# Column sums of the stick-breaking attention: operands rounded in two parts, and softplus at the end of the head's own step

## The chip, the cores and the metric

One core of one Trainium2 chip runs the whole program in one launch. The metric is the device time of an execution in microseconds, less is better. TensorE multiplies, ScalarE (ACT) evaluates functions, VectorE (DVE) does elementwise work, GpSimd (POOL) helps with small jobs, and SyncE (SP) issues the weight transfers.

## What is computed

Two blocks over 256 tokens of width 1024: an LRU layer, a sliding-window attention layer, a feed-forward layer, a mixer of MoBA and stick-breaking attention, a second feed-forward layer and a norm. The change lies in the stick-breaking attention of 8 heads:

```python
z = jnp.einsum('bhqd,bhsd->bhqs', qc, k).astype(jnp.float32) * scale
past = s_pos[None, :] < t[:, None]
log_fail = jnp.where(past, jax.nn.log_sigmoid(-z), 0.0)
later = lax.cumsum(log_fail, axis=3, reverse=True) - log_fail
w = jnp.where(past, jnp.exp(jax.nn.log_sigmoid(z) + later), 0.0)
return jnp.einsum('bhqs,bhsd->bhqd', w.astype(v.dtype), v)
```

With softplus(z) = max(z, 0) + log(1 + exp(-|z|)), the weight is exp(z - sum of softplus over the keys from s on).

## The kernel before

All weights stream through two staging buffers in halves of 128 x 1024 numbers. ScalarE rounds a half to the one-pass format fp32r (`w_hi`), VectorE makes the remainder (`w_lo`), and TensorE makes three products: hi x hi, hi x lo and lo x hi (L528: 24 instructions a half). The ring has 4 slots, so the half that is rounded after TensorE has finished half j is j + 4.

The stick-breaking heads are woven into the last sixteen halves of the mixer's input projection. A loop over steps r is written out on TensorE, ScalarE and VectorE alike. `STICK_FILL` says how many halves stand in each step (1, 2, 2, 1, 1, 2, 1, 1, 2, 1, 0, 2, 0); ScalarE and VectorE treat the halves of step r - 1 in step r. Keys lie on partitions. A head has 384 columns (`SC`): 256 queries against the first 128 keys, then the second 128 queries against the second 128 keys.

Step r on each engine, before:

- TensorE: in even steps the scores of heads r and r + 1 (L1004, L1007). Then the sums of head n = r - 2: a product of a lower triangle of ones with softplus (L1018, 384 columns) and of a square of ones with its last 128 columns (L1019), both plain fp32. They wait for softplus of head n (`sp_done`) and, since the bank is that of head n - 2, for that head's subtraction (`d_done`). In even steps from 6 on the values of heads r - 6 and r - 5. Then the step's halves.
- VectorE: the scores of head r with the mask into `stick_z(r)` (L2112); softplus of head r - 1 (L2119), which waits for ScalarE's logarithm; z less the sums of head r - 3 (L2124); then the halves' work (a projection's output, L1607, and the weight remainder, L1535), which waits for ScalarE's rounding.
- ScalarE: absolute value, exponential and logarithm of head r, the exponential of head r - 3, and the rounding of the halves (all recorded under L1055).

Each engine does its instructions in the order written; only semaphores tie them. GpSimd scales MoBA's probabilities (`normalise`, L493) ahead of this stretch. The constants lie in `con`, plain fp32, and `ones` is a square of ones.

Of the kernel before, what the change touches and what calls it, by code (L numbers as in the profile page):

```python
# [7 lines left out]
F32 = mybir.dt.float32  # L8
# [3 lines left out]
ALU = mybir.AluOpType  # L12
# [3 lines left out]
P = 128  # L16
T = 256
TB = T // P
D = 1024
KD = D // P  # L20
# [8 lines left out]
NH = 8  # L29
# [6 lines left out]
SC = T + P  # L36
# [40 lines left out]
IDENT, TRI, DIST, CMASK, SBMASK, FREQ = 0, 128, 256, 512, 768, 1152  # L77
# [20 lines left out]
def fill(counts, first, r):  # L98

    return range(first + sum(counts[:r]), first + sum(counts[:r + 1]))  # L100
# [57 lines left out]
def build(nc, I, out):  # L158
    ctx = ExitStack()
    with ctx:  # L160
        def sb(name, shape, dt=F32):
            return ctx.enter_context(nc.sbuf_tensor(name, shape, dt))

        def sem(name):
            return ctx.enter_context(nc.semaphore(name))
# [7 lines left out]
        acts = sb("acts", [P, 30, 2, T], F32R)  # L173
# [8 lines left out]
        con = sb("con", [P, N_CONST])  # L182
        ones = sb("ones", [P, P])
# [23 lines left out]
        bank = [two[b // 2][:, b % 2, :] for b in range(8)]  # L207

        def tiles(t, n=1):

            return arena[:, t:t + n, :].rearrange("p t n -> p (t n)")
# [23 lines left out]
        xn_ready, xh_ready, xl_ready = sem("xn_ready"), sem("xh_ready"), sem("xl_ready")  # L235
# [23 lines left out]
        rope_turn, rope_out = sem("rope_turn"), sem("rope_out")  # L259
        z_done, z_sb, sb_abs, sb_exp, sb_ln, sp_done, c_done, d_done, w_exp = (  # L260
            sem(n) for n in ("z_done", "z_sb", "sb_abs", "sb_exp", "sb_ln", "sp_done", "c_done", "d_done", "w_exp"))
        ym_hi, ym_lo, g_sig = sem("ym_hi"), sem("ym_lo"), sem("g_sig")
        br_done, mg_a, mg_b, mg_f, mg_hi, mg_lo = (
            sem(n) for n in ("br_done", "mg_a", "mg_b", "mg_f", "mg_hi", "mg_lo"))
# [25 lines left out]
        def score_parts(n, sinks):  # L290

            s = score_buf(n)
            return [s[:, 0:P + sinks], s[:, P + 1:SC + 1 + sinks]]
# [10 lines left out]
        def stick_z(n):  # L304

            return flat[:, 48 * T + (n % 6) * SC:48 * T + (n % 6 + 1) * SC]

        def stick_sp(n):

            return flat[:, 24 * T + (n % 2) * SC:24 * T + (n % 2 + 1) * SC]  # L310

        def stick_ln(n):

            return flat[:, 27 * T + (n % 3) * SC:27 * T + (n % 3 + 1) * SC]
# [118 lines left out]
        def _(pool):  # L433
# [55 lines left out]
            def normalise(n):  # L489

                pool.wait_ge(den_inv, n + 1)
                for q, s in enumerate(score_parts(n, 0)):
                    pool.tensor_scalar(s, s, rden[:, 2 * n + q:2 * n + q + 1], 1.0, ALU.mult, ALU.mult).then_inc(p_norm, 1)  # L493
# [22 lines left out]
                .then_inc(fin_gain_in, 16)  # L516
            for h in range(NH):
                normalise(NQ + h)


        @block.tensor
        def _(pe):
# [318 lines left out]
            def values_of_two(n, o, v, w):  # L841

                c = (n // 2 % 2) * T
                for i in range(2):
                    pe.matmul(bank[o][i * HD:(i + 1) * HD, c:c + T], v[i][0], w[i][:, 0:T], start=True, stop=False,  # L845
                              skip_group_check=True)
                for i in range(2):
                    pe.matmul(bank[o][i * HD:(i + 1) * HD, c + P:c + T], v[i][1], w[i][:, T:SC], start=False, stop=True,
                              skip_group_check=True).then_inc(o_done, 1)
# [12 lines left out]
            for r in range(NQ + LAG + 2):  # L862
# [4 lines left out]
                if r >= LAG + 2 and (r - LAG) % 2:  # L867
                    n = r - LAG - 3
# [91 lines left out]
            for j in range(12):  # L960
# [5 lines left out]
                if j in MIX_TURN:  # L966
                    n = MIX_TURN[j]
# [11 lines left out]
            for r in range(NH + LAG + 2):  # L979
                n = NQ + r  # L980
# [4 lines left out]
                if r >= LAG + 2 and (r - LAG) % 2:  # L985
                    h = r - LAG - 3
# [10 lines left out]
            for r in range(NH + 5):  # L997
                if r < NH and r % 2 == 0:
                    if r >= 2:
                        pe.wait_ge(z_sb, r)  # L1000
                    q, k = tiles(8 + r // 2), tiles(12 + r // 2)
                    for i in range(2):
                        s = slice(i * HD, (i + 1) * HD)
                        pe.matmul(bank[i][:, 0:T], k[s, 0:P], q[s, 0:T], start=True, stop=True)  # L1004
                    for i in range(2):
                        s = slice(i * HD, (i + 1) * HD)
                        pe.matmul(bank[i][:, T:SC], k[s, P:T], q[s, P:T], start=True, stop=True).then_inc(z_done, 1)  # L1007
                if r == 2:
                    pe.wait_ge(t_out, NQ + NH)
                if r == 5:  # L1010
                    pe.wait_ge(m_val, 4)
                if 2 <= r < NH + 2:
                    n = r - 2
                    pe.wait_ge(sp_done, n + 1)
                    if n >= 2:
                        pe.wait_ge(d_done, n - 1)
                    sums, sp_n = bank[2 + n % 2], stick_sp(n)
                    pe.matmul(sums[:, 0:SC], con[:, TRI:TRI + P], sp_n, start=True, stop=False, skip_group_check=True)  # L1018
                    pe.matmul(sums[:, P:T], ones[:, :], sp_n[:, T:SC], start=False, stop=True, skip_group_check=True)\  # L1019
                        .then_inc(c_done, 1)  # L1020
                if r >= 5 and r % 2 == 0:
                    h = r - 6
                    pe.wait_ge(w_exp, h + 2)
                    if h % 4 == 0:
                        pe.wait_ge(ym_lo, h // 4 + 1)
                    values_of_two(h, 6 + h // 4,
                                  [[v[:, tb * 512 + i * HD:tb * 512 + (i + 1) * HD] for tb in range(TB)] for i in (h, h + 1)],
                                  [stick_z(h), stick_z(h + 1)])
                for j in fill(STICK_FILL, 24, r):
                    mix_half(j)  # L1030
# [496 lines left out]
        def _(dve):  # L1527
            def lo(n, i=0, step=0):

                if n >= half_of(C_END):  # L1530
                    return
                src, landed, count = source(n)
                w = src.shape[-1]
                dve.wait_ge(hi_done, n + 1 + i * step)
                dve.tensor_tensor(w_lo[:, n % RING, 0:w], src, w_hi[:, n % RING, 0:w].bitcast(F32), ALU.subtract)\  # L1535
                    .then_inc(w_done, 1)
# [20 lines left out]
            def root_inv(n):  # L1557
                dve.wait_ge(std_ready, n + 1)
                dve.reciprocal(n_rstd[:, :], n_std[:, :]).then_inc(rstd_ready, 1)
# [35 lines left out]
            def roots_out(n, b=3):  # L1595

                dve.wait_ge(rb_ready, n)
                dve.tensor_copy(spread[:, :], bank[b][:, 0:T]).then_inc(rb_sb, 1)
                dve.wait_ge(rb_sb, n)
# [97 lines left out]
            for n in range(half_of(C_G)):  # L1697
                if n - 1 in x_end:
                    xb_lo(x_end[n - 1])
                if n in x_end:  # L1700
                    c = x_end[n]
                    dve.wait_ge(conv_b, 2 * c + 2)
                    for tap in range(1, CONV):
                        for m in range(2):
                            t = 2 * c + m
# [363 lines left out]
            def mix_slot(j):  # L2069

                c = j // 2
                if j == 3:
                    root_inv(3)
                if j == 4:
                    dve.wait_ge(rstd_ready, 4)
                    mix_out(0)
                    rope(0)
                    mix_out(1)
                if j == 5:
                    rope(1)  # L2080
                    roots_out(3)
                if j == 8:
                    mix_out(2)
                    rope(2)
                    mix_out(3)
                if j == 9:
                    rope(3)
                if j % 2 and c >= 6 and c not in (10, 11):
                    mix_out(c)
                lo(H_M + 4 + j)  # L2090
# [16 lines left out]
            for r in range(NH + 5):  # L2107
                if r < NH:
                    dve.wait_ge(z_done, r + 1)
                    if r >= 6:  # L2110
                        dve.wait_ge(o_done, NQ + NH + r - 5)
                    dve.tensor_tensor(stick_z(r), bank[r % 2][:, 0:SC], con[:, SBMASK:SBMASK + SC], ALU.add)\  # L2112
                        .then_inc(z_sb, 1)
                if 1 <= r <= NH:
                    n = r - 1
                    dve.wait_ge(sb_ln, n + 1)
                    if n >= 2:
                        dve.wait_ge(c_done, n - 1)
                    dve.scalar_tensor_tensor(stick_sp(n), stick_z(n), 0.0, stick_ln(n), ALU.max, ALU.add)\  # L2119
                        .then_inc(sp_done, 1)  # L2120
                if 3 <= r < NH + 3:
                    n = r - 3
                    dve.wait_ge(c_done, n + 1)
                    dve.tensor_tensor(stick_z(n), stick_z(n), bank[2 + n % 2][:, 0:SC], ALU.subtract).then_inc(d_done, 1)  # L2124
                if r >= 1:
                    for j in fill(STICK_FILL, 24, r - 1):
                        mix_slot(j)
                if r == 9:
                    branch_lo(2)
            for j in fill(STICK_FILL, 24, NH + 4):  # L2130
# [110 lines left out]
```

## Time and profile before

| | us |
|---|---|
| median of 3 runs | 810.54 (810.51 to 810.54) |
| the profiled execution | 810.75 |
| its span | 809.0 |
| TensorE busy | 796.4 |
| VectorE busy | 572.6 |
| ScalarE busy | 487.2 |
| GpSimd busy | 89.4 |

The span is that of the profiled execution; 1.75 us of its time lie around it. Busy times of matmuls overlap, since matmuls are pipelined: the time from one start to the next tells what one costs. A wait is idle time of an engine just before an instruction, put down to what released it. A plain fp32 matmul shows as two instructions, one on fp32r as one. Start times are microseconds from the start of the span.

### The profile page before, as it was taken

How to read it: one execution, taken by the hardware profiler on the slowest of the kernel's cores; microseconds unless marked ns; L12 is line 12 of the kernel's file. 1: busy time of each engine (PE TensorE's matmuls, PEld its weight loads, DVE VectorE, ACT ScalarE, POOL GpSimd, SP SyncE). 2: the span in 40 equal slices, each digit the busy share in tenths (PEclk: the TensorE clock that was granted, in tenths of full speed). 3: DMA queues.
4: the chain of work that ended last, by engine and by line, in shares of the span. 5: the costliest groups of instructions: out<-in, count | busy, mean ns of one | idle time of the engine just before them, and what ended most of it. 6: DMA issues, size and time to landing. Idle time of an engine off the chain costs nothing.

```text
span 809.0 us, 15016 instructions
## 1 busy us (share of the span) xinstructions
PE 796.4 (98%) x5557; PEld 728.5 (90%) x5557; DVE 572.6 (71%) x860; ACT 487.2 (60%) x763; POOL 89.4 (11%) x152
## 2 busy tenths in 40 slices
PE   8999999999999999999999999999999999999997
PEld 8999999988898888889998899988999888888885
DVE  5987897976687977786449655556587787877443
ACT  6779956886566655554346456655747565555343
POOL 9405100057400000000000012000000000000000
PEclk9999999999999999999999999999999999999999
DMA  8624565643355766665565545344546576665651
GB/s 266 203 93 127 166 204 183 184 139 97 105 183 156 209 185 204 184 184 196 186 181 174 171 132 163 106 146 155 163 152 181 166 227 186 181 191 181 198 181 53
DMA packets 101045, 136.31 MB, mean 169 GB/s; under 512 B 5064, under 2 KB 86400, under 8 KB 100992
## 3 DMA queue, kind: packets, MB, share of 16 engines
q1 hardware_dynamic: 99232, 133.23, 54.0%
q0 software_dynamic: 1600, 2.28, 1.0%
q8 instruction: 36, 0.59, 0.3%
q14 instruction: 17, 0.14, 0.1%
q10 hardware_dynamic: 160, 0.07, 0.0%
HBM read 134.51 MB, written 1.05 MB: 168 GB/s over the span
## 4 chain that ended last, share of the span: by engine, by line
PE 90%; DVE 5%; ACT 3%; issue 1%; DMA 0%; ACTq 0%; DVEq 0%
PE bank L528 40%; PE bank L597 17%; PE bank L594 10%; PE bank L536 8%; PE bank L641 7%; PE bank L592 2%; DVE w_lo L1535 2%; ACT w_hi L1055 1%; PE bank L825 1%; PE bank L845 1%; ACT arena L1055 1%; PE bank L838 1%; ACT acts L1055 1%; PE bank L1018 1%; DVE arena L1870 1%
## 5 line engine op out<-in xcount | busy, mean ns | idle before, releaser
L1535 DVE TENSOR_TENSOR w_lo<-stage,w_hi 128x1024 fp32r<-128x1024 f32 x249 | 303.2, 1224 | 156.6 <-ACT w_hi L1055 155.9
L528 PE MATMUL bank<-acts,w_hi 128*128 128x256 f32 (+1 forms) x1936 | 353.6, 285 | 2.1 <-DVE arena L1710 0.6
L1055 ACT ACTIVATE w_hi<-stage 128x1024 fp32r<-128x1024 f32 (+1 forms) x251 | 261.5, 1049 | 96.0 <-PE bank L528 48.5
L528 PEld LDWEIGHTS bank<-acts,w_hi 128*128 128x128 f32 x1936 | 301.2, 192 | 7.2 <-issue 4.3
L528 PE MATMUL bank<-acts,w_lo 128*128 128x256 f32 (+1 forms) x968 | 273.7, 283 | 0.0
L597 PE MATMUL bank<-acts,w_hi 128*128 128x512 f32 x616 | 217.6, 396 | 0.0
L594 PE MATMUL bank<-acts,w_lo 128*128 128x256 f32 x704 | 189.7, 280 | 0.0
L528 PEld LDWEIGHTS bank<-acts,w_lo 128*128 128x128 f32 x968 | 185.5, 192 | 0.0
L597 PEld LDWEIGHTS bank<-acts,w_hi 128*128 128x128 f32 x616 | 115.7, 188 | 25.5
L594 PEld LDWEIGHTS bank<-acts,w_lo 128*128 128x128 f32 x704 | 132.7, 188 | 3.6
L1055 ACT ACTIVATE arena<-bank 128x512 f32<-128x512 f32 (+1 forms) x79 | 44.1, 558 | 69.2 <-PE bank L597 46.4
L536 PE MATMUL bank<-w_hi,acts 128*128 128x256 f32 (+1 forms) x320 | 71.6, 319 | 0.4 <-DVE w_lo L1535 0.4
L1055 ACT ACTIVATE arena<-arena 128x512 f32<-128x512 f32 (+3 forms) x64 | 38.5, 605 | 46.9 <-DVE arena L1982 19.2
L493 POOL TENSOR_SCALAR arena<-arena,rden 128x128 f32<-128x128 f32 (+1 forms) x48 | 29.0, 616 | 293.4 <-DVE rden L1880 293.1
L1055 ACT ACTIVATE acts<-arena 128x512 fp32r<-128x512 f32 (+3 forms) x41 | 26.3, 642 | 57.5 <-DVE arena L2003 32.2
L536 PEld LDWEIGHTS bank<-w_hi,acts 128*128 128x128 f32 x320 | 52.3, 191 | 4.1 <-DVE w_lo L1535 0.5
L641 PE MATMUL bank<-w_hi,acts 128*128 128x512 f32 x176 | 54.5, 390 | 0.0
L536 PE MATMUL bank<-w_lo,acts 128*128 128x256 f32 (+1 forms) x160 | 50.4, 315 | 0.0
L1974 DVE TENSOR_TENSOR arena<-arena,bank 128x512 f32<-128x512 f32 x44 | 30.2, 686 | 23.2 <-ACT arena L1055 23.2
L641 PEld LDWEIGHTS bank<-w_hi,acts 128*128 128x128 f32 x176 | 33.0, 188 | 6.8
L1055 ACT ACTIVATE arena<-arena,ntop 128x129 f32<-128x129 f32 (+3 forms) x48 | 21.4, 448 | 21.3 <-DVE ntop L1873 21.2
L641 PE MATMUL bank<-w_lo,acts 128*128 128x512 f32 x88 | 34.2, 389 | 0.0
(188 smaller groups left out, 686.3 us busy)
## 6 DMA issues: line engine op xcount, KB each, us to landing
stage<-ffn_w_gate SPq DMA_DIRECT2D x44, 512.0 KB, 4.4
stage<-ffn_w_up SPq DMA_DIRECT2D x44, 512.0 KB, 4.5
stage<-ffn_w_down SPq DMA_DIRECT2D x44, 512.0 KB, 3.6
stage<-w_in SPq DMA_DIRECT2D x40, 512.0 KB, 3.6
stage<-a_w_in SPq DMA_DIRECT2D x24, 512.0 KB, 4.6
stage<-b_w_in SPq DMA_DIRECT2D x16, 512.0 KB, 3.8
stage<-a_w_out SPq DMA_DIRECT2D x12, 512.0 KB, 3.6
stage<-b_w_out SPq DMA_DIRECT2D x8, 512.0 KB, 3.5
```

The costliest lines, as they stand in the source:

```text
L493: pool.tensor_scalar(s, s, rden[:, 2 * n + q:2 * n + q + 1], 1.0, ALU.mult, ALU.mult).then_inc(p_norm, 1)
L528: mm = pe.matmul(dst, w[:, slot, c:c + P], a[:, k, :] if isinstance(k, int) else a[:, bass.ds(k, 1), :], start=start and n == 0, stop=stop ...
L536: mm = pe.matmul(dst, a[:, k, tb * P:(tb + 1) * P], w[:, slot, c:c + n], start=start and i == 0, stop=stop and i == 2, skip_group_check=True)
L592: pe.matmul(two[p][:, m, :], w_hi[:, half % RING, c:c + P], wide(acts[:, k, :, :]), start=True, stop=False, skip_group_check=True)
L594: mm = pe.matmul(two[p][:, m, 0:T], w_lo[:, half % RING, c:c + P], a_hi[:, k, :], start=False, stop=False, skip_group_check=True)
L597: mm = pe.matmul(two[p][:, m, :], w_hi[:, half % RING, c:c + P], wide(acts[:, k, :, :]), start=False, stop=k == KD - 1, skip_group_check=True)
L641: mm = pe.matmul(token_bank(tb, h)[:, :], a[:, k, t], w[:, slot, c], start=False, stop=w is w_hi and a is a_hi, skip_group_check=True)
L825: mm = pe.matmul(bank[i][:, c:c + w], q[r, t * T + c:t * T + c + P], k[r, 0:keys], start=True, stop=True)
L838: mm = pe.transpose(bank[2 + n % 2][:, c * P:(c + 1) * P], p[:, at:at + P], ident)
L1055: return nc.scalar.activation(out_, in_, func, **kw)
L1535: dve.tensor_tensor(w_lo[:, n % RING, 0:w], src, w_hi[:, n % RING, 0:w].bitcast(F32), ALU.subtract)\
L1974: dve.tensor_tensor(y, y, two[ffn_two(n, j, u)][:, :, 0:T], ALU.add).then_inc(ff_add, 1)
```

## The change

1. `stick_two(n)` gives two fp32r buffers of 384 columns in `acts` for each of two heads in turn. VectorE writes softplus rounded into the first (a copy) and the remainder into the second (a subtraction).
2. Softplus, copy and subtraction of head r stand at the end of VectorE's step r, behind the halves' work. Softplus of head r - 1 no longer stands behind the masking in step r.
3. TensorE makes the sums of a head from four fp32r matmuls: triangle and square by the rounded part (after `sp_hi`), then by the remainder (after `sp_lo`).
4. GpSimd makes fp32r copies of the triangle and of the ones once, behind the scaling of MoBA's first head.

```diff
+        def stick_two(n):
+
+            two_parts = acts[:, 16 + 2 * (n % 2):18 + 2 * (n % 2), :, :].rearrange("p k s t -> p (k s t)")
+            return two_parts[:, 0:SC], two_parts[:, SC:2 * SC]
+
+        tri, all_ones = acts[:, 24, 0, 0:P], acts[:, 24, 0, P:T]
...
             for h in range(NH):
                 normalise(NQ + h)
+                if h == 0:
+                    pool.wait_ge(xl_ready, KD * 5)
+                    pool.tensor_copy(tri, con[:, TRI:TRI + P]).then_inc(tri_in, 1)
+                    pool.tensor_copy(all_ones, ones[:, :]).then_inc(tri_in, 1)
...
                 if 2 <= r < NH + 2:
                     n = r - 2
-                    pe.wait_ge(sp_done, n + 1)
+                    if n == 0:
+                        pe.wait_ge(tri_in, 2)
+                    pe.wait_ge(sp_hi, n + 1)
                     if n >= 2:
                         pe.wait_ge(d_done, n - 1)
-                    sums, sp_n = bank[2 + n % 2], stick_sp(n)
-                    pe.matmul(sums[:, 0:SC], con[:, TRI:TRI + P], sp_n, start=True, stop=False, skip_group_check=True)
-                    pe.matmul(sums[:, P:T], ones[:, :], sp_n[:, T:SC], start=False, stop=True, skip_group_check=True)\
+                    sums, (sp_h, sp_l) = bank[2 + n % 2], stick_two(n)
+                    pe.matmul(sums[:, 0:SC], tri, sp_h, start=True, stop=False, skip_group_check=True)
+                    pe.matmul(sums[:, P:T], all_ones, sp_h[:, T:SC], start=False, stop=False, skip_group_check=True)
+                    pe.wait_ge(sp_lo, n + 1)
+                    pe.matmul(sums[:, 0:SC], tri, sp_l, start=False, stop=False, skip_group_check=True)
+                    pe.matmul(sums[:, P:T], all_ones, sp_l[:, T:SC], start=False, stop=True, skip_group_check=True)\
                         .then_inc(c_done, 1)
...
-                if 1 <= r <= NH:
-                    n = r - 1
-                    dve.wait_ge(sb_ln, n + 1)
-                    if n >= 2:
-                        dve.wait_ge(c_done, n - 1)
-                    dve.scalar_tensor_tensor(stick_sp(n), stick_z(n), 0.0, stick_ln(n), ALU.max, ALU.add)\
-                        .then_inc(sp_done, 1)
                 if 3 <= r < NH + 3:
                     n = r - 3
                     dve.wait_ge(c_done, n + 1)
...
                 if r >= 1:
                     for j in fill(STICK_FILL, 24, r - 1):
                         mix_slot(j)
+                if r < NH:
+                    n = r
+                    dve.wait_ge(sb_ln, n + 1)
+                    if n >= 2:
+                        dve.wait_ge(c_done, n - 1)
+                    sp_h, sp_l = stick_two(n)
+                    dve.scalar_tensor_tensor(stick_sp(n), stick_z(n), 0.0, stick_ln(n), ALU.max, ALU.add)\
+                        .then_inc(sp_done, 1)
+                    dve.wait_ge(sp_done, n + 1)
+                    dve.tensor_copy(sp_h, stick_sp(n)).then_inc(sp_hi, 1)
+                    dve.wait_ge(sp_hi, n + 1)
+                    dve.tensor_tensor(sp_l, stick_sp(n), sp_h.bitcast(F32), ALU.subtract).then_inc(sp_lo, 1)
```

VectorE in steps 3 and 4 before (a row is an instruction, `x2` two of them; L2112 masking, L2119 softplus, L2124 the subtraction of the sums, L1607 a projection's output, L1535 a weight remainder):

```order
495 L2112 TENSOR_TENSOR arena<-bank,con 128x384
496 L2119 SCALAR_TENSOR_TENSOR arena<-arena 128x384
497 L2124 TENSOR_TENSOR arena<-arena,bank 128x384
498 L1607 TENSOR_TENSOR arena<-bank,spread 128x512
499 L1535 TENSOR_TENSOR w_lo<-stage,w_hi 128x1024 x2
500 L2112 TENSOR_TENSOR arena<-bank,con 128x384
501 L2119 SCALAR_TENSOR_TENSOR arena<-arena 128x384
502 L2124 TENSOR_TENSOR arena<-arena,bank 128x384
```

The same place after (L2129 masking, L2134 subtraction of the sums, L1624 output, L1552 weight remainder, L2144 softplus, L2147 the rounding copy, L2149 its remainder):

```order
503 L2129 TENSOR_TENSOR arena<-bank,con 128x384
504 L2134 TENSOR_TENSOR arena<-arena,bank 128x384
505 L1624 TENSOR_TENSOR arena<-bank,spread 128x512
506 L1552 TENSOR_TENSOR w_lo<-stage,w_hi 128x1024 x2
507 L2144 SCALAR_TENSOR_TENSOR arena<-arena 128x384
508 L2147 CAST acts<-arena 128x384
509 L2149 TENSOR_TENSOR acts<-arena,acts 128x384
510 L2129 TENSOR_TENSOR arena<-bank,con 128x384
511 L2134 TENSOR_TENSOR arena<-arena,bank 128x384
```

Softplus went from between masking and subtraction to behind the weight remainders, with two instructions more behind it and the next masking after them.

TensorE in step 4 before, scores of heads 4 and 5 and the sums of head 2:

```order
2092 L1004 MATMUL bank<-arena 128x256 x2
2093 L1007 MATMUL bank<-arena 128x128 x2
2094 L1018 MATMUL bank<-arena,con 128x384
2095 L1019 MATMUL bank<-arena,ones 128x128
2096 L528 MATMUL bank<-acts,w_hi 128x256 x2
```

The same place after (L1016 and L1019 the scores, L1032 to L1036 the sums, L540 the projection):

```order
2096 L1016 MATMUL bank<-arena 128x256 x2
2097 L1019 MATMUL bank<-arena 128x128 x2
2098 L1032 MATMUL bank<-acts 128x384
2099 L1033 MATMUL bank<-acts 128x128
2100 L1035 MATMUL bank<-acts 128x384
2101 L1036 MATMUL bank<-acts 128x128
2102 L540 MATMUL bank<-acts,w_hi 128x256 x2
```

Two matmuls of a head's sums became four, at the same place between the scores and the step's halves.

## Rows read from the trace of the kernel before

**Rows 1.** The page: busy time of TensorE, and the chain that ended last, by engine

```profile
PE 796.4 (98%) x5557; PEld 728.5 (90%) x5557; DVE 572.6 (71%) x860; ACT 487.2 (60%) x763; POOL 89.4 (11%) x152
...
PE 90%; DVE 5%; ACT 3%; issue 1%; DMA 0%; ACTq 0%; DVEq 0%
```

**Rows 2.** Waits of TensorE from 505 to 580 us: who, for whom, total, times, longest

```profile
PEld bank L1018 <- DVE arena L2119: 1.1, 1, 1.1
PE bank L1018 <- DVE arena L2124: 0.9, 1, 0.9
```

**Rows 3.** Timeline of VectorE, 508 to 575 us: start, duration, engine, line, operation

```profile
513.15 0.56 DVE L2119 SCALAR_TENSOR_TENSOR arena<-arena 128x384 f32<-128x384 f32 x1 [1.42 <-ACT arena L1055]
...
519.07 0.56 DVE L2112 TENSOR_TENSOR arena<-bank,con 128x384 f32<-128x384 f32 x1 [2.12 <-PE bank L1007]
...
524.65 0.55 DVE L2112 TENSOR_TENSOR arena<-bank,con 128x384 f32<-128x384 f32 x1
...
530.64 0.55 DVE L2112 TENSOR_TENSOR arena<-bank,con 128x384 f32<-128x384 f32 x1
...
534.35 1.23 DVE L1535 TENSOR_TENSOR w_lo<-stage,w_hi 128x1024 fp32r<-128x1024 f32 x1 [1.63 <-ACT w_hi L1055]
535.49 0.55 DVE L2112 TENSOR_TENSOR arena<-bank,con 128x384 f32<-128x384 f32 x1
...
543.79 0.56 DVE L2112 TENSOR_TENSOR arena<-bank,con 128x384 f32<-128x384 f32 x1 [3.36 <-PE bank L848]
...
549.78 0.55 DVE L2112 TENSOR_TENSOR arena<-bank,con 128x384 f32<-128x384 f32 x1
550.25 0.55 DVE L2119 SCALAR_TENSOR_TENSOR arena<-arena 128x384 f32<-128x384 f32 x1
550.72 0.55 DVE L2124 TENSOR_TENSOR arena<-arena,bank 128x384 f32<-128x384 f32 x1
```

**Rows 4.** Timeline of ScalarE, same stretch

```profile
513.03 1.07 ACT L1055 ACTIVATE arena<-arena 128x384 f32<-128x384 f32 x2
...
514.65 1.04 ACT L1055 ACTIVATE w_hi<-stage 128x1024 fp32r<-128x1024 f32 x1
```

**Rows 5.** The chain that ended last, 500 to 585 us: start, duration, piece

```profile
526.71 2.86 PE bank L528 x24
...
534.36 0.65 PE bank L1018 x2
535.00 0.22 PE bank L1019 x2
...
541.82 0.84 PE bank L1018 x2
...
551.41 0.88 PE bank L1018 x2
```

**Rows 6.** The same view, 700 to 809 us

```profile
743.70 59.87 PE bank L641 x264
```

**Rows 7.** VectorE: one-source scalings (groups), and a dependent pair (timeline)

```profile
L1624 DVE TENSOR_SCALAR arena<-arena,n_rstd 128x256 f32<-128x256 f32 x5 | 1.8, 396 | 0.0
...
L2208 DVE TENSOR_SCALAR arena<-arena,n_rstd 128x512 f32<-128x512 f32 x2 | 1.0, 488 | 0.1
...
591.62 0.42 DVE L2154 TENSOR_TENSOR arena<-arena,bank 128x256 f32<-128x256 f32 x1 [1.22 <-PE bank L528]
592.15 0.42 DVE L2161 TENSOR_TENSOR arena<-arena 128x256 f32<-128x256 f32 x1
```

**Rows 8.** The program's end: TensorE's last matmul (timeline), the granted clock (windows)

```profile
803.16 0.39 PE L641 MATMUL bank<-w_hi,acts 128*128 128x512 f32 x1
...
core 0: us, PE busy (x) PEld busy (x) DVE busy (x) ACT busy (x) POOL busy (x), PEclk, DMA share, GB/s
...
805.00:806.00 1.00, 0.00 (x0) 0.00 (x0) 0.56 (x3) 0.72 (x1) 0.00 (x0) 0.77 0.79 293
806.00:807.00 1.00, 0.00 (x0) 0.00 (x0) 0.00 (x0) 0.00 (x0) 0.00 (x0) 0.50 0.30 113
```

**Rows 9.** Timeline of TensorE at the program's start

```profile
1.01 3.78 PE L703 MATMUL bank<-ones 128*128 128x128 f32 x16 [1.01 <-POOL half_pi L436]
```

**Rows 10.** Timeline of GpSimd, 455 to 510 us, the second scaling

```profile
476.19 0.83 POOL L493 TENSOR_SCALAR arena<-arena,rden 128x128 f32<-128x128 f32 x2 [3.15 <-DVE rden L1880]
```

More of the change, by code:

```diff
@@ L261, in build @@
             sem(n) for n in ("z_done", "z_sb", "sb_abs", "sb_exp", "sb_ln", "sp_done", "c_done", "d_done", "w_exp"))
+        sp_hi, sp_lo, tri_in = sem("sp_hi"), sem("sp_lo"), sem("tri_in")
         ym_hi, ym_lo, g_sig = sem("ym_hi"), sem("ym_lo"), sem("g_sig")
```

## Prediction

> **What bounds the kernel now.** Read the page first: TensorE is busy for 98% of the span and carries 90% of the chain that ended last [rows 1]. So an edit counts by what it does to TensorE: the work it takes off, and the waits it makes. Next, the waits of TensorE in the stick-breaking stretch (505 to 580 us): all that is there is one wait of 0.9 us at the sums of one head, noted under matmul and weight load, its end being head 4's subtraction (L2124) on VectorE [rows 2]. Third, VectorE's timeline there: VectorE and ScalarE go through the steps in lockstep. From one masking (L2112) to the next it takes 4.85 us in a step with one weight half (530.64 to 535.49) and 5.99 us with two (524.65 to 530.64) [rows 3]. In between VectorE idles 1.6 us for ScalarE, which does three functions of the head and the rounding of a half first. TensorE's own work of a step is about as long: a half is 2.87 us [rows 5].
>
> **TensorE's part.** A head's sums are two fp32 matmuls now, each two instructions: 0.65 + 0.22 = 0.87 us in a stream, 0.84 + 0.22 right behind the score matmuls [rows 5]. After, there are four one-instruction matmuls of rounded operands. Their rate is that of the main products: 2.86 / 24 = 0.119 us for 256 columns [rows 5], 59.87 / 264 = 0.227 us for 512 [rows 6]; half way, 0.173 us for 384. No row shows 128 columns of this kind. Extending the line gives 0.065; L1019's instructions take 0.22 / 2 = 0.11; four passes, as fp32 takes, would be 0.22. I take 0.11, the row with the same weights to load. A head costs 2 x (0.173 + 0.11) = 0.57 us, 0.30 us less (bounds 0.39 less and 0.08 less). If nothing else moved: 8 x 0.30 = 2.4 us off.
>
> **VectorE's part.** Each head gets a rounding copy and a subtraction, and softplus (the old L2119) moves from the next step's head, where it lay in the 1.6 us wait for ScalarE, to the end of its own step, where nothing covers it: the next masking stands behind it in VectorE's queue. The subtraction has two sources and 384 columns, as L2112 and L2119: 0.55 us, 0.47 to the next start (549.78 and its neighbours) [rows 3]. The copy has one source. The nearest rows are scalings of 256 columns, 0.396 us, and of 512, 0.488 us [rows 7]; midway is 0.44, and both also read a column of scalars, which the copy does not. I take 0.40, with 0.35 and 0.55 (a two-source operation of that width) as bounds. The three depend on each other; a dependent operation starts 0.11 us after its forerunner ends (591.62 + 0.42, then 592.15) [rows 7]. The tail of a step is T = (0.55 + 0.11) + (0.40 + 0.11) + 0.47 = 1.64 us.
>
> The Trainium skill (VectorE: DVE Perf Modes, its perf-mode tier table) says that an fp32 tensor_copy in SBUF runs at two elements a cycle. By that the copy would be about 0.36 us (an estimate), T 1.60, and the result 0.3 us lower. No row here shows a plain copy within SBUF.
>
> **Following the queue.** The first step has no weight half, so VectorE stands until ScalarE has head 0's logarithm at 513.15 [rows 3], as it does now, but with head 1's masking behind it.
> - Head 1 is masked at 513.15 + T = 514.79.
> - To head 2: masking 0.58, ScalarE's three functions and a half 513.03 to 515.69 = 2.66 [rows 4], 0.03, the remainder of a weight half 1.14 (534.35 to 535.49) [rows 3], T: 520.84, against 519.07.
> - To heads 3, 4, 5, 6 and 7: the present distances 5.58, 5.99, 4.85, 4.85 and 5.99 [rows 3], each plus T, since softplus did not lengthen a step before and the tail now does: 528.06, 535.69, 542.18, 548.67, 556.30. The distance now from head 5 to head 6 is longer, but that is a wait for TensorE's head 0 and 1 outputs, which come before 547.
> - Head 4's subtraction from the sums ends 1.02 later.
>
> That is 545.84 + 7T = 557.32 us, where it is 551.27 now (550.72 + 0.55) [rows 3]: **6.05 us later**. TensorE's sums of head 6 wait for exactly this, since they take the bank of head 4. On the way head 3's sums wait for head 1's subtraction, which ends at 535.69 + 1.02 = 536.71; TensorE would be there at 534.36 - 3 x 0.30 = 533.5 [rows 5], so it stands for 3.4 us, some 1.0 us more at head 5, and 4.0 us at head 6. The five savings before that vanish in these waits; only those of heads 6 and 7 stay, 0.60 us. Behind head 6 no wait on VectorE is left (head 7 needs head 5's subtraction at about 563, TensorE comes at 565), and everything later hangs on TensorE: 6.05 - 0.60 = **+5.45 us**.
>
> GpSimd's two casts stand behind the first head's scaling, where it now idles 3.15 us [rows 10]; each is about 0.4 us, like its 128-column scalings: nothing. The earlier release of softplus is worth nothing either: no TensorE wait ends on it. No transfer moves past another; the stage loads follow the weight remainders, still ahead of TensorE.
>
> **The clock.** At the end of the program TensorE's last matmul runs to 803.55 (803.16 + 0.39); the granted clock of 805 to 806 is 0.77 and then 0.50, the 1.2 GHz level [rows 8], so it fell some 2.0 us after TensorE went quiet. No wait of TensorE in the middle of the program is over 1 us now; the new ones are 3.4 and 4.0. So I expect a fall in them. One at head 3 is paid out of the later waits. One at head 6 is not: TensorE is then alone on the path. Its price: at the start sixteen fp32 instructions of 128 columns take 3.78 us, 0.236 each [rows 9], against 0.11 [rows 5], and the pace is full only after some 6 us. Between 0 and half of that, 3 us, I take 1.5. The Trainium skill (TensorE: Matmul & The Clock Gate, the table "Why this matters for your kernels") also warns of idle gaps between bursts of matmuls; it and the rows of the end agree.
>
> **Sum.** The profiled execution took 810.75 us, span 809.0; the median of the runs is 810.54. 810.75 + 5.45 + 1.5 = 817.7, and 817.5 against the median.
>
> **Rivals.**
> - The loop as above, but the clock holds or falls where it costs nothing: 816.0. For it: the clock stays at 1.00 through every short gap now. Against it: the end of the trace. 0.25.
> - The loop is longer: copy at 0.55 us (7 x 0.15 = 1.0 more) or a slow stretch of up to 3 us: 819 to 821. 0.12. The matmuls of 128 columns at 0.22 us belong here: 2 x 2 x 0.11 = 0.4 more.
> - The tail costs less than it adds up to: dependent starts cost 0.03 us instead of 0.11, as from ScalarE to VectorE, and ScalarE catches part of the later masking up: 811 to 814. 0.08.
> - Faster, 808.1: the steps have room for the tail, and TensorE's 2.4 us come through. The place is head 4's subtraction, the point 545.84 + 7T = 551.27 + 0.60, so T = 0.86 us. Softplus and the subtraction alone are 0.94, without copy or dependence. TensorE waits at that point already. 0.03.
> - The change doesn't do what it says: rounded operands run in four passes like fp32. Then a head costs 1.74 us, 0.87 more, of which heads 6 and 7 count, 2.3 more than in the sum: 819 to 820. Against it: 0.119 us for 256 columns. 0.04.
>
> The forecast, 817.5, has 0.48, its own range 816.5 to 819. The range 814.5 to 820.5 leaves out the cheap-tail and faster cases and the far end of the long ones. A measurement of this kernel tells about 0.2% (1.6 us) from no change: faster by more 0.03, within it 0.04, slower 0.93.
>
> **What would show it.** In the profile after: the masking's starts 6.5 us (one half) and 7.6 us (two) apart in place of 4.85 and 5.99; copy 0.40 and subtraction 0.55 us; head 4's subtraction ending about 6 us later; waits of TensorE at the first sums matmul of heads 3 and 6, 3 to 4 us each, released by VectorE's subtraction from the sums; sums of a head in 0.57 us; a granted clock below 1.00 in the slices at 535 to 565 us. It is wrong if these waits are absent (VectorE had room), if T is under 1 us, or if the clock stays 1.00, which is the first rival.

## The result

| | before | after |
|---|---|---|
| median | 810.54 us (6 runs) | 816.33 us (6 runs, 815.12 to 817.51) |
| ratio after / before | | 1.007, 95% interval 1.006 to 1.008 |
| profiled execution, span | 810.75, 809.0 us | 815.13, 813.3 us |

The kernel became 0.7% slower. TensorE's busy time rose by 0.5 us, although its added matmuls are cheaper than those removed, and the granted clock left full speed in the middle of the program. Of all the runs behind this document one, of the kernel "The old place" below, took 960.15 us at a mean granted clock of 0.753; it is left out of every median and ratio. From the page of after, the busy time and the clock in the 40 slices (the row of before has nines from end to end):

```profile
PE 796.9 (98%) x5557; PEld 730.8 (90%) x5557; DVE 579.3 (71%) x876; ACT 487.3 (60%) x763; POOL 90.2 (11%) x154
...
PEclk9999999999999999999999999989999999999999
```

VectorE's timeline in the stick-breaking stretch, after: the tail of the first step, then the masking of each head (L2129) in turn and head 4's subtraction (L2134), which answer to [rows 3]:

```profile
512.99 0.56 DVE L2144 SCALAR_TENSOR_TENSOR arena<-arena 128x384 f32<-128x384 f32 x1 [1.89 <-ACT arena L1072]
513.58 0.36 DVE L2147 CAST acts<-arena 128x384 fp32r<-128x384 f32 x1
513.97 0.56 DVE L2149 TENSOR_TENSOR acts<-arena,acts 128x384 fp32r<-128x384 f32 x1
514.45 0.55 DVE L2129 TENSOR_TENSOR arena<-bank,con 128x384 f32<-128x384 f32 x1
...
520.34 0.55 DVE L2129 TENSOR_TENSOR arena<-bank,con 128x384 f32<-128x384 f32 x1
...
527.37 0.55 DVE L2129 TENSOR_TENSOR arena<-bank,con 128x384 f32<-128x384 f32 x1
...
534.81 0.55 DVE L2129 TENSOR_TENSOR arena<-bank,con 128x384 f32<-128x384 f32 x1
...
541.11 0.55 DVE L2129 TENSOR_TENSOR arena<-bank,con 128x384 f32<-128x384 f32 x1
...
547.83 0.56 DVE L2129 TENSOR_TENSOR arena<-bank,con 128x384 f32<-128x384 f32 x1 [0.33 <-PE bank L860]
...
555.28 0.55 DVE L2129 TENSOR_TENSOR arena<-bank,con 128x384 f32<-128x384 f32 x1
555.75 0.54 DVE L2134 TENSOR_TENSOR arena<-arena,bank 128x384 f32<-128x384 f32 x1
```

The maskings of heads 2 to 5 are 7.03, 7.44 and 6.30 us apart, where they were 5.58, 5.99 and 4.85. Each step grew by 1.45 us: 0.59 for softplus, 0.39 for the copy, 0.47 for the subtraction up to the next start. Head 4's subtraction ends at 556.29 (555.75 + 0.54), 5.02 us later than before. The stretch itself began 0.17 us earlier (the first masking, not among these lines, starts at 510.55; before it was 510.72), so 5.19 us were lost up to there.

TensorE's waits on that subtraction's line (500 to 600 us: who, for whom, total, times, longest), in answer to [rows 2], and pieces of the chain, in answer to [rows 5]:

```profile
PE bank L1032 <- DVE arena L2134: 4.9, 2, 2.7
```

```profile
535.97 0.66 PE bank L1032
...
556.44 0.41 PE bank L1032
...
563.95 0.18 PE bank L1032
564.12 0.06 PE bank L1033
564.18 0.23 PE bank L1035
564.41 0.06 PE bank L1036
```

Two waits, 2.7 us at head 3 and 2.2 at head 6. A head's sums at full speed are 0.18 + 0.06 + 0.23 + 0.06 = 0.53 us (from 563.95). At head 3 the first matmul behind the wait is 0.66 us long, at head 6 0.41: at head 3 the array was slow. The windows (stretch; busy time and instructions of TensorE, its weight loads, VectorE, ScalarE, GpSimd; then the granted clock) show where:

```profile
530.00:534.00 4.00, 3.31 (x28) 3.10 (x26) 2.89 (x4) 1.99 (x3) 0.00 (x0) 1.00 0.16 32
534.00:538.00 4.00, 2.03 (x8) 2.06 (x9) 2.39 (x5) 2.54 (x5) 0.00 (x0) 0.69 0.77 245
538.00:542.00 4.00, 4.00 (x21) 4.00 (x20) 3.42 (x6) 0.79 (x2) 0.00 (x0) 0.50 0.20 54
542.00:546.00 4.00, 4.00 (x35) 3.82 (x33) 1.30 (x3) 2.72 (x5) 0.00 (x0) 0.96 0.22 77
552.00:556.00 4.00, 2.23 (x19) 2.03 (x17) 3.93 (x7) 0.60 (x2) 0.00 (x0) 1.00 0.46 144
556.00:560.00 4.00, 3.56 (x29) 3.15 (x30) 1.91 (x3) 2.89 (x5) 0.00 (x0) 1.00 0.33 120
```

TensorE stood idle from about 533.3 to 536, and the clock is 0.50 from 538 to 542, the 1.2 GHz level, with 21 matmuls in 4 us instead of some 35. In this execution the wait at head 6 (552 to 556) passed without a fall.

### The profile page after: what moved, and what is told of

Its sections match the earlier page's. It is cut to its first block, busy times and chain, and to the rows that moved or that the text cites. A ratio compares the mean times of both kernels' runs of the same rounds, so it can differ in the third digit from the quotient of the medians.

```text
span 813.3 us, 15034 instructions
## 1 busy us (share of the span) xinstructions
PE 796.9 (98%) x5557; PEld 730.8 (90%) x5557; DVE 579.3 (71%) x876; ACT 487.3 (60%) x763; POOL 90.2 (11%) x154
## 4 chain that ended last, share of the span: by engine, by line
PE 89%; DVE 6%; ACT 3%; issue 1%; DMA 0%; ACTq 0%; DVEq 0%
PE bank L540 39%; PE bank L609 17%; PE bank L606 10%; PE bank L548 8%; PE bank L653 7%; PE bank L604 2%; DVE w_lo L1552 2%; ACT w_hi L1072 1%; ACT arena L1072 1%; PE bank L837 1%; PE bank L857 1%; PE bank L850 1%; ACT acts L1072 1%; DVE arena L1887 1%; DMA rows_n<-a_norm_g 0%
## 5 line engine op out<-in xcount | busy, mean ns | idle before, releaser
L1552 DVE TENSOR_TENSOR w_lo<-stage,w_hi 128x1024 fp32r<-128x1024 f32 x249 | 302.9, 1223 | 158.6 <-ACT w_hi L1072 157.8
L540 PE MATMUL bank<-acts,w_hi 128*128 128x256 f32 (+1 forms) x1936 | 355.7, 286 | 2.0 <-DVE arena L1727 0.6
L540 PEld LDWEIGHTS bank<-acts,w_hi 128*128 128x128 f32 x1936 | 303.2, 193 | 7.1 <-issue 4.3
L540 PE MATMUL bank<-acts,w_lo 128*128 128x256 f32 (+1 forms) x968 | 274.8, 284 | 0.0
L540 PEld LDWEIGHTS bank<-acts,w_lo 128*128 128x128 f32 x968 | 186.6, 193 | 0.0
```

The costliest lines, as they stand in the source:

```text
L540: mm = pe.matmul(dst, w[:, slot, c:c + P], a[:, k, :] if isinstance(k, int) else a[:, bass.ds(k, 1), :], start=start and n == 0, stop=stop ...
```

## The experiments

Each kernel was timed beside the kernel before on the same chip; the ratios are to that. The three instructions at the end of VectorE's step (softplus, copy, remainder) are called the tail. Theory 1: what is lost is the tail, behind which the next masking queues, seven times up to head 4's subtraction, plus a fall of the clock in the waits that this makes. A run's mean clock is the granted clock over its whole span; a fall in mid-program lowers it, and so does a fall at the very end, so that the kernel before shows 0.998 to 1.000.

**Moving only.** Plain fp32 sums as before, softplus alone at the end of its own step.

```diff
-                if 1 <= r <= NH:
-                    n = r - 1
-                    dve.wait_ge(sb_ln, n + 1)
...
                     for j in fill(STICK_FILL, 24, r - 1):
                         mix_slot(j)
+                if r < NH:
+                    n = r
+                    dve.wait_ge(sb_ln, n + 1)
...
```

> The kernel before with its plain fp32 sums, softplus alone moved to the end of the head's own step. Theory 1: T is 0.47 us, head 4's subtraction could end at 545.84 + 7 x 0.47 = 549.1, earlier than 551.27, so the loop stays bound by TensorE as before: 810.5 us, within 0.5. Rival (the move by itself is what costs, by the wait for ScalarE in the first step): 812 to 814 us.

Measured: 810.64 us, ratio 1.0001 (0.9992 to 1.0009). The move by itself costs nothing; TensorE's only wait on VectorE in the stretch is still one of 0.9 us.

**The old place.** All of the rounding, at softplus's old place:

```diff
+                if 1 <= r <= NH:
+                    n = r - 1
+                    dve.wait_ge(sb_ln, n + 1)
...
+                    dve.tensor_tensor(sp_l, stick_sp(n), sp_h.bitcast(F32), ALU.subtract).then_inc(sp_lo, 1)
                 if 3 <= r < NH + 3:
                     n = r - 3
                     dve.wait_ge(c_done, n + 1)
...
-                if r < NH:
-                    n = r
-                    dve.wait_ge(sb_ln, n + 1)
...
```

> The rounded parts and the four one-pass matmuls as in the changed kernel, but softplus, copy and subtraction stand where softplus stood before, right behind the next head's masking, in VectorE's wait for ScalarE. Theory 1 (what costs is that the next masking queues behind the tail, once per step, 7T up to head 6): the maskings go back to 4.85 and 5.99 us apart, and the time is 810.5 - 0.7 = 809.8 us, with up to 1.7 more if the wait left at head 6 (2.5 us) lets the clock fall. Rival (the extra VectorE work costs wherever it stands): 815 us or more.

Measured: 811.59 us, ratio 1.0011 (1.0002 to 1.002); nine of twelve runs lie from 811.47 to 811.66, one at 810.02 and one at 812.80. So 4.7 of the 5.8 us are a matter of place. The maskings did not quite go back to the old distances. VectorE's timeline of step 4 of this kernel (L2129 masking, L2137 softplus, L2140 copy, L2142 its remainder, L2146 subtraction of the sums), and two windows behind head 6's wait:

```profile
530.82 0.55 DVE L2129 TENSOR_TENSOR arena<-bank,con 128x384 f32<-128x384 f32 x1
531.29 0.55 DVE L2137 SCALAR_TENSOR_TENSOR arena<-arena 128x384 f32<-128x384 f32 x1
531.87 0.36 DVE L2140 CAST acts<-arena 128x384 fp32r<-128x384 f32 x1
532.27 0.56 DVE L2142 TENSOR_TENSOR acts<-arena,acts 128x384 fp32r<-128x384 f32 x1
532.75 0.55 DVE L2146 TENSOR_TENSOR arena<-arena,bank 128x384 f32<-128x384 f32 x1
...
535.98 0.55 DVE L2129 TENSOR_TENSOR arena<-bank,con 128x384 f32<-128x384 f32 x1
```

```profile
552.00:554.00 2.00, 2.00 (x14) 1.43 (x13) 1.23 (x2) 0.74 (x1) 0.00 (x0) 0.63 0.23 88
554.00:556.00 2.00, 2.00 (x11) 2.00 (x11) 1.85 (x4) 0.05 (x1) 0.00 (x0) 0.52 0.36 72
```

The maskings are 5.16 us apart (530.82 to 535.98), not 4.85. The subtraction of the sums now comes behind the tail, ScalarE's exponential waits for it (0.18 us in this step), and its rounding of the half stands behind that: the cover is not wide enough by 0.3 us. This does not reach the end: head 6's masking waits for TensorE's values of heads 0 and 1 here (1.26 us) as before (3.36), and head 4's subtraction ends at 551.23, where it was 551.27. What brings the time above the kernel before is the clock: behind the wait of 2.5 us at head 6 it is 0.63 and 0.52. The run at 810.02 has a mean clock of 0.999, the nine one of 0.996 or 0.997, that at 812.80 one of 0.995. By that one run, this kernel without a fall is 0.6 us faster than the kernel before (810.63 on that chip); with it, it is 1.0 us slower.

**One place further on.** The tail behind the subtraction of the sums, ahead of the halves:

```diff
                     dve.tensor_tensor(stick_z(n), stick_z(n), bank[2 + n % 2][:, 0:SC], ALU.subtract).then_inc(d_done, 1)
+                if 1 <= r <= NH:
+                    n = r - 1
+                    dve.wait_ge(sb_ln, n + 1)
...
+                    dve.tensor_tensor(sp_l, stick_sp(n), sp_h.bitcast(F32), ALU.subtract).then_inc(sp_lo, 1)
                 if r >= 1:
                     for j in fill(STICK_FILL, 24, r - 1):
                         mix_slot(j)
```

> As e1, but softplus, copy and subtraction stand one place further on: behind the masking and the subtraction of the sums, ahead of the step's halves. Theory 1: neither the masking nor the subtraction of the sums waits for the tail, TensorE's saving comes through in part: 808.7 us, a wait of 1.7 us left at head 6, maskings 4.85 and 5.99 us apart. Rival: the tail takes time from the weight remainders behind it and TensorE waits for a half: 811 us or more.

Measured: 810.61 us, ratio 0.9994 (0.9985 to 1.0003), in two groups: three of eleven runs from 809.08 to 809.11 at a mean clock of 0.999, eight from 810.55 to 810.67 at 0.997. Two maskings one half apart, then the only wait of TensorE left on VectorE (L2144 is the rounding copy here), and two windows behind it:

```profile
530.48 0.55 DVE L2129 TENSOR_TENSOR arena<-bank,con 128x384 f32<-128x384 f32 x1
...
535.34 0.55 DVE L2129 TENSOR_TENSOR arena<-bank,con 128x384 f32<-128x384 f32 x1
```

```profile
PE bank L1032 <- DVE acts L2144: 1.5, 1, 1.5
```

```profile
550.00:552.00 2.00, 1.87 (x10) 1.15 (x12) 1.34 (x3) 1.78 (x3) 0.00 (x0) 0.75 0.74 276
552.00:554.00 2.00, 2.00 (x13) 1.67 (x10) 1.98 (x3) 0.46 (x2) 0.00 (x0) 0.50 0.03 12
```

The maskings are back at the distance of before (4.86 us, where it was 4.85), so the same 1.46 us cost nothing in this place. Even this short wait let the clock fall in the profiled execution, and a fall costs 1.5 us here (810.61 against 809.1). That was not expected: the forecast was 808.7 us, and the shortest pause I had a row for was 2.0 us.

**The clock.** 24 matmuls of 256 columns whose output nobody reads, right before the wait at the sums of head 3, of head 6, or of both (the diff shows both):

```diff
+                    if n in (3, 6):
+                        for _ in range(24):
+                            pe.matmul(bank[7][:, 0:T], tri, acts[:, 0, 0, :], start=True, stop=True, skip_group_check=True)
                     pe.wait_ge(sp_hi, n + 1)
```

> The changed kernel with 24 matmuls of 256 columns more, whose output nobody reads, right before the sums of head 3 and of head 6, so that TensorE works through 2.9 us of each long wait. Theory 1 (the spread of the changed kernel, 815.1 to 817.5, is the clock's fall in one of the two waits): clock 1.00 through the stretch, every run at 815.0 within 0.2. Rival (the spread has another cause, and the clock costs nothing): the same spread of over 2 us, or 2 x 2.9 us more.

> The changed kernel with the 24 unread matmuls only ahead of head 6's sums. Theory 1 (a fall of the clock in head 3's wait is paid out of the later waits, one in head 6's is not): every run at 814.8 to 815.2 us, with or without a fall at head 3. Rival (the fall at head 3 also counts): a spread up to 817.

> The changed kernel with the 24 unread matmuls only ahead of head 3's sums. Theory 1: head 6's wait of 3.8 us is left open, the clock falls there in most runs: 814.8 us where it does not, 816 to 817.5 where it does. Rival: steady at 815.

| unread matmuls before | median | lowest to highest, 5 runs |
|---|---|---|
| heads 3 and 6 | 814.82 us | 814.79 to 814.87 |
| head 6 only | 814.70 us | 814.63 to 814.76 |
| head 3 only | 816.49 us | 816.19 to 817.74 |
| none (the changed kernel, 6 runs) | 816.33 us | 815.12 to 817.51 |

Matmuls without use ahead of head 6's sums, with or without those at head 3, make the kernel faster by 1.5 to 1.6 us, and its five runs then lie within 0.13 us. The windows with head 6's wait filled:

```profile
534.00:538.00 4.00, 1.98 (x16) 2.01 (x17) 2.44 (x5) 2.49 (x5) 0.00 (x0) 1.00 0.78 251
...
552.00:556.00 4.00, 3.21 (x27) 3.01 (x26) 3.93 (x8) 0.60 (x2) 0.00 (x0) 1.00 0.51 174
556.00:560.00 4.00, 3.91 (x32) 3.49 (x33) 1.91 (x3) 2.54 (x5) 0.00 (x0) 1.00 0.23 90
```

and with only head 3's filled, ahead of them the waits of TensorE on VectorE in that kernel (L1035 is the first sums matmul, 3 lines further down):

```profile
PE bank L1035 <- DVE arena L2137: 4.4, 2, 3.8
```

```profile
534.00:538.00 4.00, 4.00 (x35) 4.00 (x34) 2.45 (x5) 2.45 (x5) 0.00 (x0) 1.00 0.79 251
...
552.00:556.00 4.00, 0.34 (x3) 0.14 (x2) 3.93 (x8) 0.60 (x2) 0.00 (x0) 0.99 0.57 175
556.00:560.00 4.00, 3.89 (x17) 2.98 (x18) 1.91 (x3) 2.56 (x5) 0.00 (x0) 0.50 0.24 89
560.00:564.00 4.00, 4.00 (x26) 4.00 (x25) 2.39 (x5) 1.47 (x2) 0.00 (x0) 0.66 0.46 131
```

Head 6's open wait is 3.8 us there, and the clock is 0.50 from 556 to 560. Filled, it stays 1.00. So a fall at head 6 costs 1.5 to 3.0 us where it comes (816.19 and 817.74, against 814.70). The runs of that kernel fit in the mean clock too: 0.997 from 816.19 to 816.49, 0.995 at 817.72 and 817.74.

With head 6's filled and head 3's open no run is over 814.76. In the profiled execution of that kernel the clock held at head 3 (534 to 538), and four of its five runs have a mean clock of 0.999, so the case of a fall at head 3 with head 6's wait filled was hardly tested. What such a fall costs is told by the changed kernel itself: its profiled execution has one and is among its lowest, 0.4 us above 814.70. Its head 6 masking then waited 0.33 us for TensorE's values of heads 0 and 1 (547.83 above).

The spread of the changed kernel is then a matter of where the clock falls. All its six runs have the same mean clock, 0.995, yet go from 815.12 to 817.51, 0.4 to 2.8 us above 814.70; the median is 1.6 above. That fits a fall at head 3 in the lowest and at head 6 in the others. But the one execution of it that was profiled fell at head 3; for the others the place is inferred, not seen.

**The length of the tail.** Once without the remainder (no subtraction, and its two matmuls left out, so a part of the computation is missing; the diff shows VectorE's part), once with the copy made twice:

```diff
-                    dve.wait_ge(sp_hi, n + 1)
-                    dve.tensor_tensor(sp_l, stick_sp(n), sp_h.bitcast(F32), ALU.subtract).then_inc(sp_lo, 1)
```

```diff
                     dve.wait_ge(sp_done, n + 1)
+                    dve.tensor_copy(sp_l, stick_sp(n))
                     dve.tensor_copy(sp_h, stick_sp(n)).then_inc(sp_hi, 1)
```

> The changed kernel without the remainder of softplus: no subtraction, and the two matmuls of it left out, so that a part of the computation is missing. The tail is 0.59 + 0.28 = 0.87 us. Theory 1 (time goes as 7 tails up to head 6): 7 x (1.46 - 0.87) = 4.1 us less than the changed kernel without a fall of the clock, 815.1 - 4.1 = 811.0, up to 2 more where the clock falls in head 6's wait. Rival (the loss is mostly one shift in the first step, where VectorE stands for the logarithm): 814 us.

> The changed kernel with the rounding copy made twice (the first into the remainder's buffer, overwritten afterwards). The tail grows by a copy's start distance of 0.28 us. Theory 1: 7 x 0.28 = 2.0 us more: 817.1 us at the least and up to 819.5 with the clock's fall. Rival: 0.3 us more or nothing, VectorE having 29% idle time.

Measured: 811.55 us without the remainder (ratio to before 1.0013, 1.0004 to 1.0022) and 818.41 with the second copy (1.0098, 1.0084 to 1.0111; lowest run 816.62). First and last masking of each, from VectorE's timeline:

```profile
510.67 0.55 DVE L2126 TENSOR_TENSOR arena<-bank,con 128x384 f32<-128x384 f32 x1
...
550.84 0.55 DVE L2126 TENSOR_TENSOR arena<-bank,con 128x384 f32<-128x384 f32 x1
```

```profile
510.84 0.55 DVE L2129 TENSOR_TENSOR arena<-bank,con 128x384 f32<-128x384 f32 x1
...
557.04 0.55 DVE L2129 TENSOR_TENSOR arena<-bank,con 128x384 f32<-128x384 f32 x1
```

From head 0's masking to head 7's it is 40.17 us without the remainder, 44.73 in the changed kernel, 46.20 with the second copy. The tails are 0.60 us shorter and 0.27 longer; seven of them are 4.2 less and 1.9 more. Found are 4.56 less and 1.47 more; what differs is 0.36 and 0.42. Neither kernel waits at head 6's masking, while in the changed kernel that wait put it off by 0.42 us (541.11 to 547.83 is 6.72, not 6.30). Without it the loop goes as seven tails, both ways, within 0.1 us.

The times bear it out. From the 814.70 without a fall, 1.9 more is 816.6, and the lowest run is 816.62; the expectation's "at the least 817.1" had started from 815.12, which holds a fall at head 3. The other way, 4.2 for the tails and 2 x 0.29 for the matmuls left out at heads 6 and 7 give 809.9; measured is 811.55, at mean clocks of 0.995 to 0.998 in all eleven runs, so one fall of 1.6 us would close the sum. The profiled execution (812.98) shows such a fall at head 6.

**A kernel that gains.** The tail as in the last place, and one half of the projection moved from step 8 to step 7, so that real work stands where the wait was; and the same half moved in the kernel before:

```diff
-STICK_FILL = [1, 2, 2, 1, 1, 2, 1, 1, 2, 1, 0, 2, 0]
+STICK_FILL = [1, 2, 2, 1, 1, 2, 1, 2, 1, 1, 0, 2, 0]
```

> As e4, and one half of the projection stands in step 7 instead of step 8, so that TensorE has 2.87 us of real work ahead of head 6's sums. Theory 1 (e4's 809.1 and 810.6 us are one wait of 1.6 us at head 6 and the clock's fall in it): the wait goes, no fall, 809.1 - 1.6 - up to 0.6 = 806.5 to 807.5 us in every run. Rival (the half moves the wait to another place, or VectorE's step 8 with its two halves becomes the bound): 808.5 us or more.

> The kernel before with only the same half moved from step 8 to step 7. Theory 1: its one wait of 0.9 us goes, 809.5 us; the gain of e7 over this one, some 3 us, is then TensorE's saving on the sums (8 x 0.34 = 2.7 us). Rival: most of e7's gain comes from the moved half alone: 807 to 808 us.

Measured: 807.04 us with the rounded sums, ratio 0.9961 (0.9948 to 0.9975), four of five runs from 807.00 to 807.06, one at 808.68 with a mean clock of 0.999, as high as that of the others (0.998 to 0.999), so not by the clock; 809.40 us for the kernel before with the half moved, ratio 0.9985 (0.9976 to 0.9994). The chain of the former has no wait at head 6 (551.43); the two halves ahead of it and the sums:

```profile
545.63 5.80 PE bank L540 x48
551.43 0.18 PE bank L1032
551.61 0.06 PE bank L1033
551.67 0.23 PE bank L1035
551.89 0.06 PE bank L1036
```

The half alone brings 1.2 us: its wait of 0.9 us, and the first sums matmul behind it, which takes 0.65 us in the stream instead of 0.88. The rounded sums bring a further 2.4 us, of the 8 x 0.34 = 2.7 that they save on TensorE (some 3 were expected). This version beats both kernels.

## Why the prediction was right, point by point

The time forecast was 817.5 us in a range of 814.5 to 820.5; it is 816.33. The direction and the mechanism held: VectorE's queue, with the next masking behind the tail, not TensorE's matmuls, sets the end of the stretch.

- **TensorE's part.** Forecast 0.57 us for a head's sums, measured 0.53. A 128-column matmul takes 0.06, the extension of the line, not the 0.11 I took; but the 384 columns behind it take 0.23 instead of 0.18. The pair is 0.29, where I had 0.28. The saving is 0.34 us a head instead of 0.30. The prediction speaks of five savings that vanish before head 6; there are six, heads 0 to 5. The sum has only those of heads 6 and 7 and is not touched by that.
- **The tail.** T was mis-sized: 1.64 us forecast, 1.46 measured. Two terms were off. A dependent instruction on VectorE starts 0.03 us after the end of its forerunner (512.99 + 0.56, then 513.58), not 0.11; the row I had taken reads `bank`, TensorE's output memory, and whether that makes the difference was not tested. And the copy is 0.36 us, not 0.40. The Trainium skill (VectorE: DVE Perf Modes, its perf-mode tier table) was right on that one: an fp32 copy within SBUF at two elements a cycle gives some 0.36 us (an estimate), and the trace agrees with 0.36.
- **Following the queue.** With T = 1.46 the formula 545.84 + 7T gives 556.06; less the earlier start of 0.17 and with the 0.42 by which the wait at head 6's masking put it off it is 556.31, measured 556.29. That wait I had ruled out, since I let a slow clock at head 3 be paid out of TensorE's waits alone. In this execution it also delayed the values of heads 0 and 1. The two experiments on the length of the tail bear the seven out.
- **What is left at the end.** The sum had +5.45 us without the clock. The profiled execution is 4.38 us above that of before (815.13 - 810.75), the filled kernel 4.2 above the median (814.70 - 810.54).
- **The clock.** Forecast a fall at head 6 for 1.5 us; the filled kernels show 1.6 in the median, and 0.4 to 3.0 in single runs. The 1.5 was the middle between nothing and 3 us, so that it came out so well is in part luck: single runs lie near both ends. In the profiled execution the fall is at head 3 and not at head 6. Luck also lies in the 2.0 us after which the clock fell at the end of the kernel before: at the end of the changed kernel TensorE's last matmul ends before 808 us, and the clock is still 1.00 up to 812. The prediction lets the Trainium skill (TensorE: Matmul & The Clock Gate, "Why this matters for your kernels") and the rows of the end agree; they do in kind, but its warning is for longer gaps than the 1.5 us that were enough here, and the measurement decides. The waits were forecast as 3.4 us at head 3, 1.0 at head 5 and 4.0 at head 6. They are 2.7 at head 3, shorter by four tails of 0.18 less each; where head 3's is filled, 0.6 at head 5 and 3.8 at head 6; and in the changed kernel's profiled execution none at head 5 and 2.2 at head 6, since TensorE came later by its slow stretch.
- **Rivals.** That the clock holds was the first, at 816.0. It gave the right time to 0.3 us for the wrong reason: without a fall the kernel is at 814.7. The sum was 1.2 us too high in the loop and right on the clock. Of the rival with a cheap tail (811 to 814) one half came true, the dependent starts at 0.03 us; it is worth 7 x 0.16 = 1.1 us. The other half did not: ScalarE caught nothing up, each step grew by the whole tail. The loop was not longer than forecast either, though in single runs a fall cost 3 us. The tail fits no gap, and a head's sums take 0.53 us, not the 1.74 of four passes.
- **Faster from T = 0.86 on.** The kernel without the remainder has T = 0.86, and the formula holds: head 4's subtraction ends at 551.84 us (551.30 + 0.54), 551.86 by the sum. Its time is 811.55, yet 1 us above before. The point left out the clock: at that T TensorE waits 3.2 us at head 6. And the kernel is no clean case of the point, since it also leaves out two matmuls a head.

What stays open: when a wait lets the clock fall, and how long it then stays low in a given run. No experiment here steers that. Nor does the clock explain every run: the run at 808.68 us (above) lies 1.6 us over its fellows at no lower a mean clock.

## What to carry to other kernels

Where two engines go through a loop in lockstep, count what stands behind each instruction in its queue: 1.46 us at the end of a step cost 1.45 us a step; the same instructions ahead of the halves' work, in the wait for the other engine, cost none. A busy share of 71% says nothing on that. And when a change makes the bounding engine wait, price the clock with it. Sometimes it is worth more to move a piece of real work into the wait: here one half in `STICK_FILL` made 807.04 us of 810.61.

## What was not expected of the hardware

A wait of TensorE of 1.5 us was enough for the granted clock to fall to 0.50, in eight of eleven runs by their times and mean clocks, and one such fall cost 1.5 us; 24 matmuls without use ahead of a wait made a kernel 1.6 us faster. The length of a wait alone does not decide: in the kernel with the second copy the one at head 6 took 2.9 us and passed at full clock. Two windows of that execution, the first without a matmul:

```profile
556.00:558.00 2.00, 0.00 (x0) 0.00 (x0) 1.97 (x6) 0.38 (x1) 0.00 (x0) 1.00 1.07 346
558.00:560.00 2.00, 1.80 (x14) 1.38 (x15) 0.65 (x2) 1.94 (x5) 0.00 (x0) 1.00 0.39 154
```

And where one-pass matmuls of 384 and 128 columns with different weights alternate, the short one takes 0.06 us and the long one behind it 0.23 instead of 0.18, so a short matmul is not as cheap as its own row says.
